# The first norm's factors in a transfer of their own, and the forget gates' weights split into one tile: what it does to the start of a two-block transformer kernel

## The reference

```python
h = rms_norm(x, mix_norm_pre[layer])
proj = jnp.einsum("bsd,de->bse", h, w_in[layer])
xa, ga, q, k, v, f_logit, g_a, g_b = jnp.split(proj, offs, axis=-1)
xc = causal_dwconv(xa, conv_a_w[layer], conv_a_b[layer])     # 1,280 channels, 4 taps
...
cum = jnp.cumsum(jax.nn.log_sigmoid(f_logit.astype(jnp.float32)), axis=1)   # 16 heads, f_logit + b_forget
```

## Time and profile before

| | us |
|---|---|
| time, median of 3 runs (lowest to highest) | 1196.15 (1195.58 to 1196.34) |
| the profiled execution, its own time | 1196.31 |
| its span, first to last instruction | 1194.5 |
| PE busy | 1170.8 (98%) |
| DVE busy | 910.9 (76%) |
| ACT busy | 710.5 (59%) |
| POOL busy | 379.3 (32%) |

### The profile page before, as it was taken

How to read it: one execution, slowest core, us unless ns; L and a number is a source line. 1 busy time by engine, 2 the same in 40 slices (tenths; PEclk the granted TensorE clock), 3 DMA queues, 4 the chain that set the end, 5 groups by cost and what they waited for, 6 DMA issues and landing times.

```text
span 1194.5 us, 23920 instructions
## 1 busy us (share of the span) xinstructions
PE 1170.8 (98%) x8502; PEld 1099.6 (92%) x8502; DVE 910.9 (76%) x1346; ACT 710.5 (59%) x1129; POOL 379.3 (32%) x397
## 2 busy tenths in 40 slices
PE   8999999999999999998999999999999999999996
PEld 8999989999899999888999988888899999888886
DVE  7866897867699998548898698777666768877754
ACT  6598655554467777445754566666555556666552
POOL 3444000700445555222000135545320006555431
PEclk9999999999999999999999999999999999999999
DMA  6556433376546555562534256556765435655661
GB/s 214 180 191 215 139 124 108 125 269 188 193 119 184 188 178 184 205 193 85 182 107 138 72 161 209 186 184 200 257 196 191 142 111 181 203 179 189 207 201 69
DMA packets 56627, 204.47 MB, mean 171 GB/s; under 512 B 6688, under 2 KB 6840, under 8 KB 56432
## 3 DMA queue, kind: packets, MB, share of 16 engines
q1 hardware_dynamic: 54288, 197.35, 51.1%
q0 software_dynamic: 1696, 5.13, 1.2%
q10 hardware_dynamic: 576, 1.05, 0.2%
HBM read 202.43 MB, written 2.63 MB: 172 GB/s over the span
## 4 chain that ended last, share of the span: by engine, by line
PE 90%; DVE 7%; ACT 1%; DMA 1%; issue 0%; POOL 0%; DVEq 0%; SPq 0%; POOLq 0%; ACTq 0%
PE bank L1382 20%; PE bank L1388 15%; PE bank L1389 14%; PE bank L1390 14%; PE bank L1383 11%; PE bank L1652 2%; PE bank L1385 2%; PE bank L1489 2%; PE bank L1490 2%; PE bank L1491 2%; DVE w_lo L679 2%; DVE h_two L709 1%; PE bank L1576 1%; DVE work L834 1%; DVE work L733 1%; PE bank L1566 1%
## 5 line engine op out<-in xcount | busy, mean ns | idle before, releaser
L679 DVE TENSOR_TENSOR w_lo<-raw,w_hi 128x1024 fp32r<-128x1024 f32 x374 | 477.7, 1284 | 130.2 <-ACT w_hi L276 125.2
L276 ACT ACTIVATE w_hi<-raw 128x1024 fp32r<-128x1024 f32 x374 | 392.0, 1052 | 136.4 <-PE bank L1390 66.0
L1388 PE MATMUL bank<-h_two,w_hi 128*128 128x256 f32 x1184 | 342.4, 289 | 11.4 <-DVE h_two L709 7.5
L1389 PE MATMUL bank<-h_two,w_hi 128*128 128x256 f32 x1184 | 335.6, 283 | 0.0
L1390 PE MATMUL bank<-h_two,w_lo 128*128 128x256 f32 x1184 | 335.5, 283 | 0.0
L1388 PEld LDWEIGHTS bank<-h_two,w_hi 128*128 128x128 f32 x1184 | 227.5, 192 | 17.9 <-issue 9.0
L1389 PEld LDWEIGHTS bank<-h_two,w_hi 128*128 128x128 f32 x1184 | 227.8, 192 | 0.3
L1390 PEld LDWEIGHTS bank<-h_two,w_lo 128*128 128x128 f32 x1184 | 227.6, 192 | 0.0
L1382 PE MATMUL bank<-h_two,w_hi 128*128 128x512 f32 x616 | 221.5, 398 | 1.0 <-DVE h_two L709 1.0
L1383 PE MATMUL bank<-h_two,w_lo 128*128 128x256 f32 x704 | 183.6, 281 | 0.0
L1382 PE MATMUL bank<-u_two,w_hi 128*128 128x512 f32 x455 | 161.0, 397 | 0.0
(11 more groups left out here) (244 smaller groups left out, 1851.8 us busy)
## 6 DMA issues: line engine op xcount, KB each, us to landing
raw<-in_stream SPq DMA_DIRECT2D x374, 512.0 KB, 3.6
bias_rows<-bias_row POOLq DMA_DIRECT2D x1, 1536.0 KB, 15.2
work<-in_x_t SPq DMA_DIRECT2D x2, 512.0 KB, 6.2
work<-in_x_t POOLq DMA_DIRECT2D x1, 1024.0 KB, 5.7
work<-bias_rows POOLq DMA_DIRECT2D x1, 1024.0 KB, 11.1
out<-work ACTq DMA_DIRECT2D x4, 256.0 KB, 2.4
work<-in_lmask POOLq DMA_DIRECT2D x1, 512.0 KB, 7.3
work<-bias_rows POOLq DMA_DIRECT2D x1, 512.0 KB, 6.5
```

The costliest lines, as they stand in the source:

```text
L276: A(w_hi[:, slot, :], raw[:, slot, :], ACT.Copy).then_inc(hi_ready, 1)
L679: v.tensor_tensor(w_lo[:, slot, :], raw[:, slot, :], w_hi[:, slot, :].bitcast(F32), ALU.subtract).then_inc(lo_ready, 1)
L1388: mm(out, w_hi[:, slot, s], r_two[:, 0, :], start=start, stop=False)
L1389: mm(out, w_hi[:, slot, s], r_two[:, 1, :], start=False, stop=False)
```

## The change

The first norm's gain, the first 8 columns of `par`, is a transfer of its own, with a semaphore of its own (`gain_in`), and the other 377 columns are issued behind x's second half and weight part 1. POOL's five transfers wait for x's second half. DVE's preparations of the second block's gates (`stage_parameters`, three small operations) and of the forget gates' weights (`forget_weights`) leave the start: the first goes behind the forget gates' result, the second into the last pair of `xa` tiles. The table product for the position bias (L1516, `ext_mm`) moves from ahead of tile 2 to ahead of tile 5 on PE, and its copy on ACT from the first to the third pair. The forget gates' weights lie in one tile as high, high, low (3 x 16 columns for each of 8 input tiles), so that one matmul of 48 columns multiplies both parts with `h_hi`; the result comes in two bands of partitions, 0 to 15 and 32 to 47, which DVE adds: 16 matmuls in place of 24, and three DVE operations in place of one.

```diff
-        WF_HI, WF_LO = (u[:, 2 * R + 2, 0:C * H_FOX] for u in (u_hi, u_lo))
+        WF_TWO = u_two[:, 2 * R + 2, :, :].rearrange("p z t -> p (z t)")[:, 0:3 * C * H_FOX].rearrange(
+            "p (c z f) -> p c z f", c=C, z=3)
...
-            sp.dma_start(par[:, :], par_d).then_inc(par_in, 16)
+            sp.dma_start(par[:, 0:C], par_d[:, 0:C]).then_inc(gain_in, 16)
             for n in range(RING):
...
                 sp.dma_start(raw[:, n, :], stream[n]).then_inc(landed[n], 16)
+                if n == 1:
+                    sp.dma_start(par[:, C:NCOL], par_d[:, C:NCOL]).then_inc(par_in, 16)
...
-            act.wait_ge(par_in, 16)
+            act.wait_ge(gain_in, 16)
...
             rms("mix")
+            act.wait_ge(par_in, 16)
...
-                if p == 0:
+                if p == 2:
                     act.wait_ge(ext_mm, 1)
...
-            dve.wait_ge(par_in, 16)
+            dve.wait_ge(gain_in, 16)
             for c in range(C):
                 h_low("mix", c)
                 if c % 4 == 3:
                     lo(0, 0, c // 4)
-
-            l0, l1 = (par[:, COLS["lb"] + C * r:COLS["lb"] + C * r + C] for r in range(2))
-            chain.wait(v.tensor_tensor(der[:, D_LB:D_LB + C], l0, l1, ALU.max))
...
-            dve.wait_ge(wf_in, 16)
-            v.tensor_copy(WF_HI, wf[:, :]).then_inc(wf_split, 1)
-            dve.wait_ge(wf_split, 1)
-            v.tensor_tensor(WF_LO, wf[:, :], WF_HI.bitcast(F32), ALU.subtract).then_inc(wf_split, 1)
             lo(0, 0, 2)
             step("xa", 0)
             rstd("mix")
+            dve.wait_ge(par_in, 16)
...
+            def forget_weights():
+                dve.wait_ge(wf_in, 16)
+                w = wf[:, :].rearrange("p (c o f) -> p c o f", c=C, o=1)
+                v.tensor_copy(WF_TWO[:, :, 0:2, :], w.to_broadcast([P, C, 2, H_FOX])).then_inc(wf_split, 1)
+                dve.wait_ge(wf_split, 1)
+                v.tensor_tensor(WF_TWO[:, :, 2:3, :], w, WF_TWO[:, :, 0:1, :].bitcast(F32),
+                                ALU.subtract).then_inc(wf_split, 1)
...
                 if p == 3:
                     columns(1)
+                if p == R // 2 - 1:
+                    forget_weights()
...
+                    for k in range(2):
+                        rows = slice(32 * k, 32 * k + H_FOX)
+                        v.tensor_tensor(att_s[0:H_FOX, k, 0:S], bank[7][rows, 0:S], RSTD[rows, :],
+                                        ALU.mult).then_inc(f_part, 1)
+                    dve.wait_ge(f_part, 2)
+                    v.tensor_tensor(att_s[0:H_FOX, 0, 0:S], att_s[0:H_FOX, 0, 0:S], att_s[0:H_FOX, 1, 0:S],
+                                    ALU.add).then_inc(f_normed, 1)
+                    stage_parameters()
...
+            pool.wait_ge(x_in[1], 16)
             pool.dma_start(onehot, onehot_d).then_inc(tab_in, 16)
...
             pe.wait_ge(wf_split, 2)
             for c in range(C):
-                ws, out = slice(c * H_FOX, (c + 1) * H_FOX), bank[7][0:H_FOX, 0:S]
-                mm(out, WF_HI[:, ws], h_hi[:, c, :], start=(c == 0), stop=False)
-                mm(out, WF_HI[:, ws], h_lo[:, c, :], start=False, stop=False)
-                last = mm(out, WF_LO[:, ws], h_hi[:, c, :], start=False, stop=(c == C - 1))
+                both = WF_TWO[:, c, :, :].rearrange("p z f -> p (z f)")
+                if c >= 1:
+                    mm(bank[7][0:H_FOX, 0:S], WF_TWO[:, c, 0, :], h_lo[:, c, :], start=False, stop=False)
+                last = mm(bank[7][0:3 * H_FOX, 0:S], both, h_hi[:, c, :], start=(c == 0), stop=(c == C - 1))
+                if c == 0:
+                    mm(bank[7][0:H_FOX, 0:S], WF_TWO[:, c, 0, :], h_lo[:, c, :], start=False, stop=False)
             last.then_inc(f_mm, 1)
```

More of the change, by code:

```diff
@@ L161, in build @@
         x_in = [sem(f"x_half_in{i}") for i in range(2)]
-        par_in, wf_in, tab_in, cst_in, x_back, lm_in, bias_in = (
-            sem(n) for n in ("par_in", "wf_in", "table_in", "const_in", "x_back", "lmask_in", "bias_in"))
+        par_in, gain_in, wf_in, tab_in, cst_in, x_back, lm_in, bias_in = (
+            sem(n) for n in ("par_in", "first_gain_in", "wf_in", "table_in", "const_in", "x_back", "lmask_in", "bias_in"))
         row_out, ext_out, out_done = sem("bias_row_out"), sem("bias_rows_out"), sem("out_done")
@@ L201, in build @@
         low_out, half_added = sem("low_half_out"), sem("half_added")
+        f_part = sem("forget_part_normed")
         square_done, b_done, gelu_done = (sem(n) for n in ("decay_squared", "b_done", "gelu_done"))
@@ L747, in _ @@
                     lo(0, 0, c // 4)
-            l0, l1 = (par[:, COLS["lb"] + C * r:COLS["lb"] + C * r + C] for r in range(2))
-            chain.wait(v.tensor_tensor(der[:, D_LB:D_LB + C], l0, l1, ALU.max))
-            for r, l in enumerate((l0, l1)):
-                v.tensor_tensor(der[:, D_E + C * r:D_E + C * r + C], l, der[:, D_LB:D_LB + C],
-                                ALU.subtract).then_inc(der_ready, 1)
-            dve.wait_ge(wf_in, 16)
-            v.tensor_copy(WF_HI, wf[:, :]).then_inc(wf_split, 1)
-            dve.wait_ge(wf_split, 1)
-            v.tensor_tensor(WF_LO, wf[:, :], WF_HI.bitcast(F32), ALU.subtract).then_inc(wf_split, 1)
             lo(0, 0, 2)
@@ L761, in _, with stage_parameters @@
             rstd("mix")
+            dve.wait_ge(par_in, 16)
+            def stage_parameters():
+                l0, l1 = (par[:, COLS["lb"] + C * r:COLS["lb"] + C * r + C] for r in range(2))
+                chain.wait(v.tensor_tensor(der[:, D_LB:D_LB + C], l0, l1, ALU.max))
+                for r, l in enumerate((l0, l1)):
+                    v.tensor_tensor(der[:, D_E + C * r:D_E + C * r + C], l, der[:, D_LB:D_LB + C],
+                                    ALU.subtract).then_inc(der_ready, 1)
+            def forget_weights():
[5 more added lines that the diff above has]
+                                ALU.subtract).then_inc(wf_split, 1)
             for p in range(R // 2):
@@ L815, in _ @@
                     dve.wait_ge(f_mm, 1)
-                    v.tensor_tensor(att_s[0:H_FOX, 0, 0:S], bank[7][0:H_FOX, 0:S], RSTD[0:H_FOX, :],
-                                    ALU.mult).then_inc(f_normed, 1)
+                    for k in range(2):
[6 more added lines that the diff above has]
+                    stage_parameters()
             for n in range(8):
@@ L1513, in _ @@
             pair_stat("mix")
-            pe.wait_ge(tab_in, 32)
-            mm(bank[5][0:H_MOBA, 0:EXT], table, onehot, start=True, stop=True).then_inc(ext_mm, 1)
             for t in range(2, R):
+                if t == 5:
+                    pe.wait_ge(tab_in, 32)
+                    mm(bank[5][0:H_MOBA, 0:EXT], table, onehot, start=True, stop=True).then_inc(ext_mm, 1)
                 if t == 6:
```

## The result

| | before | changed |
|---|---|---|
| median, us (lowest to highest of 6) | 1196.14 (1195.58 to 1196.34) | 1201.07 (1200.63 to 1201.19) |
| ratio to before, 95% interval | | 1.0041 (1.0030 to 1.0051) |
| span of the profiled execution, us | 1194.5 | 1199.3 |

The account below looks back on a forecast made before the run. TensorE, busy 98% of the span, was taken to bound the kernel, so the start of v's first matmul decides. The terms -3.0 + 4.9 - 0.9 + 1.6 = +2.6 us gave 1198.7 us, range 1196.5 to 1200.8.

Parts of the forecast that it names:

- 8 matmuls fewer, and the clock: Forget gates on TensorE: 16 matmuls for 24 save 0.9 us, the low clock behind the wait adds 1.6.
- -3.0 us from x to S: At the start: x lands earlier, so the statistic ends at 16.8 us instead of 19.81, a gain of 3.0 us.
- The landing of x: x's second half at the start: lands at 7.7 us, between 7.0 and 9.1, instead of 10.14.
- early bound: x's second half lands at 7.0 us, from issue, fixed 1.9 us and three 512 KB transfers at 403 GB/s.
- POOL's chain of sums: POOL's sums of squares ahead of the statistic: 5.1 us from first to last sum, as before.
- worth nothing: Start on VectorE: removing three small operations and two on wf gains nothing, since it waited for the root anyway.
- +4.9 us of wait: TensorE waits 4.9 us ahead of the forget gates for VectorE to split their weights; all of v queues behind.
- "+1.6 us" for the clock: Behind the forget gates' wait: clock falls to 1.2 GHz for some 3.4 us of work, costing 1.6 us (0 to 2.4).
- Rival 1: The clock stays up through the forget gates' wait: +1.0 us, 1197.2 us; chance 0.22.
- Rival 2: Start: transfers don't get out of each other's way, x lands at 9.1 or 9.7: 1200.1 to 1200.8 us; chance 0.16.
- main case: Whole kernel: slower by 2.6 us, 1198.7; own range 1197.9 to 1199.7 with x between 7.0 and 8.4; chance 0.57.
- Nothing for each: par's rest, moved table product and its copy cost nothing; likewise the added operations on VectorE in v.

Follow-up runs that it names:

- experiment 5: Changed kernel without POOL's wait for x's second half, so its five transfers are issued at the start beside x: 1201.45 us.
- experiment 6: Changed kernel with forget weights split ahead of the reciprocal, plus par's 377 other columns issued ahead of x again: 1196.33 us.
- experiment 2: Kernel before, with only the two operations splitting the forget gates' weights moved on VectorE into the last pair of xa tiles: 1203.36 us, ratio 1.0058.
- experiment 7: Changed kernel with forget weights split ahead of the reciprocal, and VectorE's low parts of weight parts 2 and 3 behind POOL's sums: 1194.55 us, ratio 0.9988.
- early: Changed kernel with the forget gates' weights split in VectorE's idle time ahead of the reciprocal: 1195.15 us, ratio 0.9990; looked at again once, 1195.51.
- experiments 3, 4 and 7: First two: changed kernel with 32, then 20, output-less ones-tile products on TensorE ahead of its wait for the forget weights: 1201.65, then 1199.04 us.
- columns behind: Early kernel with the first norm's 8 columns issued behind x's first half: 1195.5, 1195.66, 1195.3 us; fourth profile, also with low parts behind POOL's sums, 1194.76.

## Why the prediction was wrong

The sign and the mechanism were right; two terms of the sum were mis-sized, both to the same side. In the prediction's order, S being the end of the statistic:

| term | forecast | measured | from |
|---|---|---|---|
| start to S | -3.0 | -1.15 | S at 18.66 for 19.81 |
| wait | +4.9 | +4.8 | 47.98 - 18.66 against 44.33 - 19.81 |
| 8 matmuls fewer, and the clock | +0.7 | +1.24 | 3.44 for 2.73, and 0.53 in `v` |
| sum | +2.6 | +4.9 | |

S is taken from the chain in order of time of the changed kernel (start, us, what):

```profile
15.55 2.36 POOL work L1246 x2
...
17.95 0.71 PE bank L1456 x2
18.66 0.02 issue
```

**"-3.0 us from x to S"** is the step that failed, by 1.85 us. *The landing of x* was taken at 7.7 and was 8.54: 0.8. The prediction placed its estimate nearer to the early end because most of the slack lay behind POOL's issues. But, by single profiles, POOL's transfers cost 0.75 us in all (experiment 5), no more than the 0.9 that their 369 KB take at 403 GB/s and that the early bound had already left out: none of the slack was theirs. `par`'s bytes cost 1.1 instead of 0.5 (experiment 6), so 0.6 of the 2.1 us of slack went with them, and the other 1.5 stayed (8.54 against the early bound of 7.0). Why x's two halves and part 0 took longer than their bytes stays open. *POOL's chain of sums* was carried over as 5.1 us and became 5.9: 0.8. The prediction said of VectorE's small operations that they are "worth nothing", as VectorE waits there anyway. They were worth something to POOL, since what moved up in their place is work that holds POOL back (experiment 2: 6.0 us with two of them taken away; experiment 7: 4.1 us with no low part beside the last three sums). *The last product* behind the sums took 0.77 instead of 0.6.

The same step let the first weight product start at about 8.3 us. It took the early bound of the first half's landing, 4.4, for its value; the half came at 5.9, and the product at 9.90. That cost nothing at S, as TensorE still waited 1.0 us for POOL there, and the clock stayed at 1.00 through the start, as forecast.

The prediction weighed the rule of the Trainium skill (DMA: Bandwidth & Descriptors, Specifications) that transfers of under 512 bytes are read, modified and written, and let it change the sum only past 3.6 us. The small transfer landed in 1.8 us, within the bound. What is queued behind it did come later: x's first half takes about 1 us longer from issue to landing than with nothing ahead (4.4 to 4.7 us against 3.4 to 3.7). But behind all of `par`, in rows of 1,540 bytes, it took 4.4 and 4.8, so no run here shows that the small rows are the reason.

**"+4.9 us of wait"** was right: 4.8. So were its parts (copy 0.28, difference 0.69, VectorE without a gap from the reciprocal on) and the claim that all of `v` queues behind it.

**"+1.6 us" for the clock** was right in kind and 0.4 too small: 2.03 with the wait filled. It lasted for 4.7 us of work instead of 3.4. Rival 1, the clock staying up, fell.

**Rival 2** (x's landing at 9.1 or later) came half true at 8.54, but the range's upper end, 1200.8, was built from this one error with all others at their middle. The measured 1201.07 has three smaller errors of one sign: 0.8 at the landing, 0.8 in POOL's sums, 0.5 in the clock. (The main case's own range doesn't follow from its condition: by the prediction's sum, x between 7.0 and 8.4 gives 1198.0 to 1199.4, not 1197.9 to 1199.7. Nothing else hangs on it.) *Nothing for each* of the moved table product, its copy, the wait for `par`'s rest and the added operations behind `v` holds: from `v` to the end both kernels run alike (the first statistic behind it starts at 335.18 before and at 340.07 now, 288.12 and 288.65 us after `v`'s first product, and the 0.53 between them are the slow products; from there to the end it is 859.3 and 859.2).

## What to carry to other kernels

Work that feeds the engine which never waits must be done by the time that engine passes; when you move it later "to where it is needed", add up what the producing engine still has queued ahead of it. VectorE's idle time ahead of the reciprocal cost nothing; behind the last pair's other work it was 4.8 us late, and the clock's fall added 2 more. And when small operations are taken out of an idle stretch, look at what moves up into their place and whom it meets there.

## What the hardware showed that was not expected

**The same idle time sometimes drops the clock.** The prediction took from the earlier trace rows that 1.98 us of waiting leaves the clock up. In the changed kernel the same wait of the same length came 4.9 us later, and the clock fell behind it:

```profile
331.28 0.35 PE L1407 MATMUL bank<-h_two,w_hi 128*128 128x256 f32 x1 [1.98 <-DVE h_two L714]
```

```profile
330.00:332.50 2.50, 0.98 (x7) 0.81 (x7) 2.50 (x5) 1.63 (x4) 1.79 (x2) 1.00 0.00 0
332.50:335.00 2.50, 2.50 (x12) 2.50 (x13) 2.50 (x7) 1.61 (x4) 0.93 (x1) 0.55 0.00 0
```

The kernel before has 1.00 over that place (325 to 332.5). It cost nothing there, since TensorE was waiting for VectorE anyway: by the chain the reciprocal ahead of this place starts 4.88 us later than before (325.45 for 320.57), and the statistic behind it too (340.23 for 335.35). The long wait for the forget gates' weights shows the same. In the changed kernel the clock fell 2.7 us after the last product. In experiment 2, in a wait of 4.58 us, it was 1.00 up to 49.5, 4.2 us after the last product; in experiment 5, in one of 4.64 us, it was 1.00 up to 48.5 and fell only when the gates had begun at 48.74. The low clock then lasted for 3.1 and 3.6 us of work, not 4.7. What decides when it falls no run here shows.

**What stands ahead of x at the start costs more than its bytes.** From issue to landing, us:

| kernel | ahead of x | beside it | x's first half issued at | it took | second half took |
|---|---|---|---|---|---|
| changed | 4 KB | | 1.20 | 4.7 | 6.4 |
| early, and again | 4 KB | | 1.20 | 4.7, 4.6 | 6.3, 6.5 |
| experiments 3, 4 and 7 | 4 KB | | 1.20 | 4.7, 4.7, 4.4 | 6.4, 6.4, 6.2 |
| experiment 5 | 4 KB | POOL's 369 KB | 1.20 | 4.8 | 7.1 |
| experiment 6 | 4 KB and 188.5 KB | | 1.67 | 4.7 | 7.4 |
| before | 192.5 KB | POOL's 369 KB | 1.20 | 4.4 | 8.0 |
| experiment 2 | 192.5 KB | POOL's 369 KB | 1.20 | 4.8 | 8.3 |
| columns behind (four profiles) | nothing | | 0.76 | 3.4 to 3.7 | 5.7 to 7.1 |

The first half takes 4.4 to 4.8 us whether 4 KB or 192.5 KB stand ahead of it, and about 1 us less when nothing does. At the second half POOL's transfers cost 0.7 us and `par`'s bytes 1.1 (0.5 at 403 GB/s), and the two together 1.6 to 1.9: here the prices add up. With nothing ahead the second half spreads over 1.4 us, so the order of the small transfer makes no difference there that could be told from chance. What makes the first microseconds of the queue slow (209 GB/s from 2 to 4 us in the changed kernel) stays open.
